# Running maximum of the gated memory spread by one-pass products of split halves; token scales turned to columns through all 128 rows

## The chip, the cores and the metric

One core of one Trainium2 chip. The metric is device microseconds of one execution, the median of three runs. The kernel runs a whole two-part transformer forward pass over 512 tokens; nothing is left to the host but laying the data out.

## The reference, cut to what matters

The first block is an attention block with a feed-forward part, the second block (run twice, layers `l` = 0 and 1) has a SwiGLU part, a mixer of three branches, and another SwiGLU part. The change touches two things in it.

The gated memory (`_mlstm`, 4 heads of 128 channels) is a causal product with gates. Per head and token there is an input gate `ig` and a log forget gate `lf`. With `F` the running sum of `lf`, the weight of key token s for query token t is

```
exp(ig[s] - F[s] - max over u <= t of (ig[u] - F[u], 0))
```

so each head needs the running maximum `M[t]` of `a = ig - F`, and it needs it for every one of the 128 partitions that hold key tokens, along a free axis of 512 query tokens.

The token scales are `rsqrt(mean(x*x) + eps)` of a normalisation, one number per token. In the kernel activations lie with channels on partitions and tokens on the free axis, except for the attention values, which lie with tokens on partitions. There the same scale is needed as a column, `[128 tokens, 1]` for each of the four token blocks.

## The kernel before

Everything is float32. Large products are made of two rounded halves: a weight block and an activation are each a high half and a low half of type fp32r (which TensorE takes in one pass), and three one-pass products (high·high, high·low, low·high) accumulate in one PSUM bank. Products of plain float32 operands leave two matmul records each in the trace, transposes one.

The weights come in 386 units of 8 blocks of 128x128 over one queue (SyncE). For each unit ScalarE makes the high half (L1679, one 128x1024 instruction) and GpSimd the low half (L1992, four 128x256 instructions), two units ahead at most. TensorE walks through the blocks in the order of `plan()`.

The order of all engines' instructions is written by a planner at build time. `Schedule.put` appends a step to one list and also runs it on five model clocks (`class Planned`), with a price for each instruction. Small chains (an attention item, a normalisation) are generators that yield what they wait for; `Schedule.pump` advances one when the planned time of what it waits for has come, and so its TensorE steps land between the steps of a dense group. The prices that matter here: a matmul is 0.013 us plus 0.00167 us a column for float32 and 0.000417 us a column for fp32r, a transpose is 0.11 us. Every engine then issues its own instructions in the order of that list and waits at semaphores where the data isn't there.

The parts that the change touches:

- `columns` (TensorE, matmuls through L721 as all `mm`; VectorE copy L1127) turns a row into columns. The scale tile has the same row in all 128 partitions; the step reads partition 0 alone, four products of `[1,128]` by `[1,1]`. It is called six times: twice at the start (`("rc", 1)`, `("rc", 2)`; the second with a strided view, every fourth token), once in each mixer for the value scale (`("rc", s)`), and once in each mixer for the low-rank branch (`("low", l)`).
- `fgate_in`, `fgate_log`, `fgate_max` (VectorE, L1439 to L1458) work on 4 partitions, one a head: the gate, the two scans, the maximum `Mr` in tile T[3]. `fgate_out` transposes `a` and `M + F` to columns, `fgate_cols` copies them (L1468).
- `ml_m` (TensorE) spreads row h of `Mr` over 128 partitions with a float32 product: stationary `sel_t[0:4, ...]`, which has -1 in row h, moving `Mr`, 4 rows by 512. VectorE copies the bank (L1551) and ScalarE exponentiates. It runs four times in each mixer: heads 0 and 1 one right behind the other, heads 2 and 3 later, each when the PSUM pair of an earlier head has been read (`ml_open`, L1615).
- `sel_t` is loaded once with the second block's masks; it shares its memory with a mask of the first block.

Of the kernel before, what the change touches and what calls it, by code (L numbers as in the profile page):

```python
# [8 lines left out]
F32R = mybir.dt.float32r  # L9
# [6 lines left out]
S = 512  # L16
# [491 lines left out]
def build_program(nc, w, xT, cols, pos, c128, dmask, smask, cmask, sel, vbias, out, stop=None):  # L508
# [5 lines left out]
    with st:  # L514
# [50 lines left out]
        sel_t = at(top[0] + 2 * KB, 512)  # L565
        top[0] += 4 * KB
        R0 = top[0]
        top[0] += 110 * KB
# [18 lines left out]


        SUMS = {n: banks_t[:, 0:512 // n, 512 - n:512] for n in (128, 256)}

        def pair(slot):
            return 2 + 2 * slot, 3 + 2 * slot
# [48 lines left out]
        KR, KRT, KRS = SM[64:128, :], L1[64:128, :], L2[64:128, :]  # L641
        fz, fq = L1[0:4, :], L2[0:4, :]
        lf, Fr, zeros = PADT[0:4, 0:512], PADT[0:4, 512:1024], PAD2[0:4, 0:512]
        ar, FM, Mr = L1[0:4, :], L2[0:4, :], L3[0:4, :]
        acol, fcol = small_t[:, 32:48], small_t[:, 48:64]

        MLS = [[small_t[:, o + 4 * k:o + 4 * k + 4] for k in range(6)] for o in (64, 88)]
# [65 lines left out]
        def tensor_program(pe, need):  # L713
# [82 lines left out]
            def columns(name, b, o, src, view, dst, tok):  # L796

                need.wait_ge(*tok[0].at(tok[1]))
                if o == 0:
                    free(b)  # L800
                    bank[b] = [(v_norm, ("cols", name))]
                for c in range(4):
                    ins = mm(B[b][:, o + c:o + c + 1], view(src, c)[0:1], C["ones"][0:1, 0:1])
                ins.then_inc(*t_stat.next(("cols", name)))

            def head_sum(hid):
# [206 lines left out]
            def ml_m(l, h):  # L1013
                ba = pair(ml_at[l, h][0])[0]
                need.wait_ge(*v_attn.at(("fgate_m", l)))
                need.wait_ge(*in_cm.at("cm"))
                free(ba)
                mm(B[ba], sel_t[0:4, 128 * h:128 * h + 128], Mr).then_inc(*t_attn.next(("ml_m", l, h)))
                bank[ba] = [(v_attn, ("ml_m", l, h))]

            def ml_scores(l, h, j):
# [41 lines left out]
        def vector_program(v, need):  # L1063
# [61 lines left out]
            def columns(name, b, o, src, view, dst, tok):  # L1125
                need.wait_ge(*t_stat.at(("cols", name)))
                v.tensor_copy(dst, B[b][:, o:o + 4]).then_inc(*v_norm.next(("cols", name)))  # L1127

            def turns1():
                need.wait_ge(*in_const.at("const"))  # L1130
                need.wait_ge(*in_cols.at("cols"))
                for k in (1, 2):
                    v.tensor_reduce(SIGN[k], C[f"perm{k}"], AX, A_, negate=True).then_inc(*v_norm.next(("signs",)))
                for n, width in GAINS:
                    v.tensor_scalar(col(n), col(n), -0.5 / width, None, M_).then_inc(*v_norm.next())
                need.wait_ge(*v_norm.last())
                for n, width in GAINS[:4]:
                    v.stream_shuffle(TURNED[n], col(n), SHUFFLE[1]).then_inc(*v_norm.next(("turns1",)))

            def turns2():  # L1140
                for n, width in GAINS[4:]:
# [311 lines left out]

            def fgate_max(l):
                need.wait_ge(*v_attn.at(("fgate_a", l)))
                v.tensor_tensor_scan(Mr, ar, ar, 0.0, MX, MX).then_inc(*v_attn.next(("fgate_m", l)))
                need.wait_ge(*v_attn.last())
                v.tensor_tensor(FM, Mr, Fr, A_).then_inc(*v_attn.next(("fgate_f", l)))  # L1458

            def fgate_out(l, slot):  # L1460
                fgate_bank[l] = pair(slot)[0]
# [162 lines left out]
            def merge2(l, m, gs, tl, bz):  # L1624
# [13 lines left out]
                else:  # L1638
# [4 lines left out]
            return {"whalf": half_weights, "norm": norm, "norm_halves": norm_halves, "norm_squares": norm_squares, "stats": stats, "cols": columns, "turns1": turns1, "turns2": turns2,  # L1643
                    "rope_angles": rope_angles, "values1": values1, "proj": proj, "head_in": head_in, "key_rope": key_rope,
                    "head_rope": head_rope, "head_newton": head_newton, "dil_soft": dil_soft, "dil_norm": dil_norm,
                    "dil_pt": dil_pt, "swa_soft": swa_soft, "swa_norm": swa_norm, "swa_out": swa_out,
                    "halves1": halves1, "merge1": merge1_, "res": residual, "part": part, "relu2": relu2,
                    "relu2_halves": relu2_halves, "ff_a": ff_a, "ff_g": ff_g, "values2": values2,
                    "sb_keep": sb_keep, "sb_split": sb_split, "sb_sum": sb_sum, "sb_out": sb_out,
                    "fgate_in": fgate_in, "fgate_log": fgate_log, "fgate_max": fgate_max, "fgate_out": fgate_out,  # L1650
                    "stats_beside": stats_beside, "consts": consts, "values1_strided": values1_strided,
                    "values2_ml": values2_ml,
                    "fgate_cols": fgate_cols, "low_halves": low_halves, "low_rs": low_rsqrt, "conv": conv, "kup": kup,
# [324 lines left out]
        def pool_program(p, need):  # L1978

            def half_weights(u):  # L1980
                if u not in FRONT:
                    low_quarters(u, range(4))

            def half_weights_rest(u):
                low_quarters(u, (2, 3))

            def low_quarters(u, quarters):
                need.wait_ge(*w_high.at(u))
                hl = whl[u % 2]
                for q in quarters:  # L1990
                    c = slice(256 * q, 256 * q + 256)
                    p.tensor_tensor(hl[:, 1024:2048][:, c], wraw[u % 3][:, c], as_f32(hl[:, c]),  # L1992
                                    ALU.subtract).then_inc(*w_low.next((u, q)))

            def head_out(hid):
                H = heads[hid]
                a, b_, c = H["tiles"][H["slot"]]
                need.wait_ge(*v_attn.at(("normed", hid)))
                need.wait_ge(*H["base"][0].at(H["base"][1]))
                p.tensor_tensor(H["R"], b_, a, ALU.mult).then_inc(*p_attn.next(("head", hid)))  # L2000

            def low_squares(l):
                cq = branch[l]["cq"]
                reach(need, cq[0], *branch[l]["lay"])
                p.tensor_tensor(LS1, YL[0], YL[0], ALU.mult).then_inc(*p_attn.next())
                reach(need, cq[1])
                p.tensor_tensor(LS2, YL[1], YL[1], ALU.mult).then_inc(*p_attn.next())
                need.wait_ge(*p_attn.last())
                p.tensor_tensor(LS1, LS1, LS2, ALU.add).then_inc(*p_attn.next(("low_q", l)))
                need.wait_ge(*p_attn.last())  # L2010
                reach(need, cq[2])
                p.tensor_tensor(LS2, YL[2], YL[2], ALU.mult).then_inc(*p_attn.next(("low_kv", l)))

            return {"whalf": half_weights, "whalf_rest": half_weights_rest, "head_out": head_out, "low_squares": low_squares,
                  "mark": lambda name: mark_of("p", name)}


# [141 lines left out]
        def values_item(slot):  # L2159
            yield "t", (v_norm, ("acc", 0, 7))  # L2160
            put("mark", ("stats", 0))
            put("stats_beside", 0, 128)
            yield "t", (v_norm, ("rstd", 0))
            put("cols", ("rc", 1), 0, 384, rstdB, natural, rcol_t[:, 0:4], (v_norm, ("rstd", 0)))
            put("cols", ("rc", 2), 1, 384, rstdB, strided, rcol_t[:, 4:8], (v_norm, ("rstd", 0)))
            yield "v", (t_stat, ("cols", ("rc", 2)))
            put("values1")
            yield "v",
            put("rope_angles", 1)
            yield "a", (v_norm, ("coangle", 1))  # L2170
            put("rope_table", 1)
# [199 lines left out]
        def swiglu(l, k):  # L2371
# [4 lines left out]
            for i in range(11):  # L2376
                b1, b2 = sch.bank(), sch.bank()
                g1 = sch.dense("fa", b1, xmov(s), freed=(v_evac, ("ff_a", l, k, i)))
                if i == 0:
                    g2 = sch.dense("fg", b2, xmov(s), before=due(s), freed=(v_evac, ("ff_g", l, k, i)))  # L2380
                a, c = sch.tile(), sch.tile()
                put("ff_a", l, k, i, g1, a, busy(a, ((v_evac, ("ff", l, k, i)),)))
                if i:
                    g2 = sch.dense("fg", b2, xmov(s), freed=(v_evac, ("ff_g", l, k, i)))
                if l == 0 and k == 1 and i == 3:
                    put("rope_angles", 2)
                    put("rope_table", 2)
                    put("turns2")
                put("ff_g", l, k, i, g2, a, c, busy(c, ((v_evac, ("ff_y", l, k, i)),)))
                movs.append((HF[i][:, 0:S], HF[i][:, S:2 * S], (v_evac, ("ff", l, k, i))))  # L2390
            put("explog")
# [3 lines left out]
        def mixer(l):  # L2395
# [9 lines left out]
            put("mark", ("stats", s))  # L2405
            put("stats_beside", s, 256)

            def values_item(slot):
                yield "t", (v_norm, ("rstd", s))
                put("cols", ("rc", s), 0, 256, rstdB, natural, rcol_t[:, 0:4], (v_norm, ("rstd", s)))  # L2410
                yield "v", (t_stat, ("cols", ("rc", s)))
                put("values2", l)

# [51 lines left out]
            def gate_item(slot):  # L2465
# [5 lines left out]
                put("fgate_max", l)  # L2471
                yield "t", (v_attn, ("fgate_f", l))
                put("fgate_out", l, slot)
                yield "v", (t_attn, ("fgate", l))
                put("fgate_cols", l)

            def low_item(slot):
# [8 lines left out]
                yield "a", (t_attn, ("low_kv", l))  # L2486
                put("low_rs", l)
                yield "t", (v_attn, ("low_kv", l))
                put("cols", ("low", l), pair(slot)[0], 0, RKV, natural, rcol_t[:, 4:8], (v_attn, ("low_kv", l)))
                sch.done.add(("low", l))  # L2490

            conv_busy, n_conv = {7: lay, 8: lay, 9: lay}, [0]
# [376 lines left out]
```

## Time and profile before

| | us |
|---|---|
| median of 3 runs | 2406.74 |
| lowest and highest | 2405.58, 2408.32 |
| profiled execution, span from first to last instruction | 2406.4 |
| PE busy in it | 2379.8 |
| PEld (weight loads, beside PE) | 1924.6 |
| POOL busy | 1316.2 |
| DVE busy | 1209.2 |
| ACT busy | 965.8 |

The profile gives the profiled execution by its span; the median of the timed runs is 0.3 us above it. PE is TensorE's matmuls, PEld its weight loads, DVE is VectorE, ACT is ScalarE, POOL is GpSimd, SP is SyncE. Busy is the union of an engine's instructions in time. A matmul record is longer than the step to the next one, since matmuls overlap in the array; what a product costs is the step from one start to the next.

### The profile page before, as it was taken

How to read it: one execution, taken by the hardware profiler on the slowest of the kernel's cores; microseconds unless marked ns; L12 is line 12 of the kernel's file. 1: busy time of each engine (PE TensorE's matmuls, PEld its weight loads, DVE VectorE, ACT ScalarE, POOL GpSimd, SP SyncE). 2: the span in 40 equal slices, each digit the busy share in tenths (PEclk: the TensorE clock that was granted, in tenths of full speed). 3: DMA queues.
4: the chain of work that ended last, by engine and by line, in shares of the span. 5: the costliest groups of instructions: out<-in, count | busy, mean ns of one | idle time of the engine just before them, and what ended most of it. 6: DMA issues, size and time to landing. Idle time of an engine off the chain costs nothing.

```text
span 2406.4 us, 29717 instructions
## 1 busy us (share of the span) xinstructions
PE 2379.8 (99%) x11108; PEld 1924.6 (80%) x11108; DVE 1209.2 (50%) x1961; ACT 965.8 (40%) x1513; POOL 1316.2 (55%) x1589
## 2 busy tenths in 40 slices
PE   8999999999999999999999999999999999999999
PEld 8777778888888888777787888888887777788887
DVE  5997765423224432379625743333325785266331
ACT  4554444322223223566524432332336764344321
POOL 5763246656556655366244765555554562466554
PEclk9999999999999999999999999999999999999999
DMA  5321123333333333222122333333332221223333
GB/s 166 109 71 53 47 77 97 96 97 97 97 97 110 97 97 103 71 72 69 54 87 79 97 97 97 96 97 97 97 98 67 72 78 53 88 87 98 96 97 96
DMA packets 59758, 213.40 MB, mean 89 GB/s; under 512 B 6624, under 2 KB 6752, under 8 KB 59488
## 3 DMA queue, kind: packets, MB, share of 16 engines
q1 hardware_dynamic: 59472, 211.38, 29.2%
q8 instruction: 88, 1.44, 0.2%
q14 instruction: 54, 0.44, 0.1%
q10 hardware_dynamic: 144, 0.14, 0.0%
HBM read 209.39 MB, written 2.10 MB: 88 GB/s over the span
## 4 chain that ended last, share of the span: by engine, by line
PE 91%; DVE 6%; issue 1%; ACT 1%; DMA 0%; POOL 0%; SPq 0%; DVEq 0%; ACTq 0%
PE banks L721 89%; DVE t L1203 1%; DVE t L1211 1%; DVE t L1213 1%; DVE t L1488 1%; DVE t L1204 1%; DVE t L1197 1%; DVE t L1219 0%; PE banks L841 0%; PE banks L995 0%; DVE t L1222 0%; ACT t L1679 0%; DMA t<-in_w 0%; PE banks L875 0%; POOL t L1992 0%
## 5 line engine op out<-in xcount | busy, mean ns | idle before, releaser
L721 PE MATMUL banks<-t,t 128*128 128x512 f32 (+4 forms) x10788 | 2351.7, 387 | 17.2 <-ACT t L1699 5.9
L721 PEld LDWEIGHTS banks<-t,t 128*128 128x128 f32 (+2 forms) x10788 | 1889.5, 188 | 452.2 <-issue 64.3
L1992 POOL TENSOR_TENSOR t<-t,t 128x256 fp32r<-128x256 f32 x1544 | 1258.9, 846 | 1049.9 <-ACT t L1679 1041.5
L1679 ACT ACTIVATE t<-t 128x1024 fp32r<-128x1024 f32 x385 | 408.2, 1060 | 1078.8 <-issue 605.5
L1197 DVE TENSOR_TENSOR t<-banks,t 128x512 f32<-128x512 f32 x121 | 83.1, 687 | 169.8 <-PE banks L721 169.2
L1378 DVE TENSOR_TENSOR t<-banks,t 128x512 f32<-128x512 f32 x44 | 30.4, 690 | 184.5 <-PE banks L721 184.3
L1346 DVE SCALAR_TENSOR_TENSOR t<-banks,t 128x512 f32<-128x512 f32 x32 | 22.1, 691 | 155.4 <-PE banks L721 155.4
L1080 DVE SCALAR_TENSOR_TENSOR t<-t,t,t 128x512 fp32r<-128x512 f32 x64 | 52.0, 817 | 58.1 <-ACT t L1699 58.1
L1323 DVE TENSOR_TENSOR t<-t,t 128x512 fp32r<-128x512 f32 x68 | 70.5, 1036 | 2.3
L1352 DVE TENSOR_TENSOR t<-banks,t 128x512 f32<-128x512 f32 x24 | 16.6, 691 | 106.0 <-PE banks L721 106.0
L1699 ACT ACTIVATE t<-t,t 128x512 fp32r<-128x512 f32 x64 | 45.6, 715 | 55.7 <-DVE t L1346 49.1
L2000 POOL TENSOR_TENSOR t<-t,t 128x512 f32<-128x512 f32 x33 | 49.6, 1506 | 29.7 <-DVE t L1222 29.7
L1373 DVE TENSOR_TENSOR t<-banks,t 128x512 f32<-128x512 f32 x44 | 30.4, 691 | 70.3 <-PE banks L721 69.9
L1093 DVE TENSOR_TENSOR t<-t,t 128x512 f32<-128x512 f32 x56 | 59.4, 1061 | 3.1 <-ACT t L1705 3.1
L1321 DVE CAST t<-t 128x512 fp32r<-128x512 f32 x68 | 55.3, 813 | 2.5
L1358 DVE SCALAR_TENSOR_TENSOR t<-banks,t 128x512 f32<-128x512 f32 x32 | 22.1, 691 | 65.2 <-PE banks L721 65.1
L1344 DVE TENSOR_TENSOR t<-banks,t 128x512 f32<-128x512 f32 x32 | 22.1, 690 | 56.6 <-PE banks L721 56.6
L1488 DVE SCALAR_TENSOR_TENSOR t<-t,t,t 128x511 f32<-128x511 f32 (+2 forms) x48 | 46.7, 972 | 7.1 <-ACT t L1887 6.3
L1715 ACT ACTIVATE t<-t 128x512 f32<-128x512 f32 x45 | 28.5, 633 | 33.4 <-DVE t L1213 32.5
L1710 ACT ACTIVATE t<-banks,t 128x512 f32<-128x512 f32 x45 | 30.6, 681 | 22.5 <-PE banks L721 22.4
L1098 DVE SCALAR_TENSOR_TENSOR t<-banks,t 128x512 f32<-128x512 f32 x12 | 8.3, 692 | 57.8 <-ACT t L1715 57.7
L1705 ACT ACTIVATE t<-t 128x512 f32<-128x512 f32 x56 | 34.6, 617 | 4.8 <-DVE t L1093 4.8
(182 smaller groups left out, 1304.7 us busy)
## 6 DMA issues: line engine op xcount, KB each, us to landing
t<-in_w SPq DMA_DIRECT2D x386, 512.0 KB, 3.5
t<-in_xT SPq DMA_DIRECT2D x8, 256.0 KB, 5.7
out<-t SPq DMA_DIRECT2D x8, 256.0 KB, 4.5
t<-in_dmask SPq DMA_DIRECT2D x1, 1536.0 KB, 7.7
t<-in_vbias SPq DMA_DIRECT2D x2, 384.0 KB, 4.1
t<-in_c SPq DMA_DIRECT2D x1, 576.0 KB, 8.6
t<-in_w SPq DMA_DIRECT2D x2, 256.0 KB, 3.9
t<-in_pos SPq DMA_DIRECT2D x2, 256.0 KB, 4.1
```

What stands on the lines that cost most here:

```text
L721: return pe.matmul(o, l, r, start=start, stop=stop, skip_group_check=True)
L1080: v.scalar_tensor_tensor(out=XL[m], in0=X[m], scalar=g, in1=as_f32(XH[m]), op0=M_, op1=S_).then_inc(*v_norm.next(("xl", s, m)))
L1093: v.tensor_tensor(acc, acc, sqt, A_).then_inc(*v_norm.next(("acc", s, m)))
L1197: v.tensor_tensor(G.dst, B[G.bank], rstdB, M_).then_inc(*v_evac.next(("proj", g)))
L1321: v.tensor_copy(hi, src).then_inc(*v_evac.next())
L1323: v.tensor_tensor(lo, src, as_f32(hi), S_).then_inc(*v_evac.next(name))
L1488: v.scalar_tensor_tensor(out=dst[:, tap:S], in0=T[k][:, 0:S - tap], scalar=cols_t[:, cw + 3 - tap:cw + 4 - tap], in1=dst[:, tap:S], op0=M_ ...
L1679: a.activation(whl[u % 2][:, 0:1024], wraw[u % 3][:, :], ACT.Copy).then_inc(*w_high.next(u))
L1699: a.activation(XH[m], X[m], ACT.Copy, scale=col(STAGE[s], m)).then_inc(*a_norm.next(("high", s, m)))
L1705: a.activation(sqt, X[m], ACT.Square).then_inc(*a_norm.next(("square", s, m)))
L1992: p.tensor_tensor(hl[:, 1024:2048][:, c], wraw[u % 3][:, c], as_f32(hl[:, c]), ALU.subtract).then_inc(*w_low.next((u, q)))
L2000: p.tensor_tensor(H["R"], b_, a, ALU.mult).then_inc(*p_attn.next(("head", hid)))
```

## The change

`Mr` is no longer read by TensorE. VectorE rounds it to fp32r into rows 0 to 3 of a new 128-row tile `Mhl` and writes the remainder to rows 32 to 35 (`fgate_halves`); the other 120 rows are zeroed by GpSimd once in each mixer (`fgate_zero`). `sel` is copied to rows 32 to 35 as well and rounded to fp32r in place, once (`select`, VectorE, in the first SwiGLU part behind `turns2`). `ml_m` is then one fp32r product of 128 rows, which adds high and low half. `Mr` moves to the tile that held `lf`, `Mhl` takes the place of T[3].

`columns` reads all 128 rows. For the two calls at the start (result one column wide) it is a float32 product with the first column of the identity as moving operand; for the other four it is a transpose of the 128x128 block, of which VectorE copies the first column.

```diff
+        TURNS = banks_t[:, 0:4, 256:384]
+        def few(b):
+            return B[b][:, 384:388].rearrange("p (c n) -> p c n", c=4)
+        def whole(b):
+            return B[b].rearrange("p (c n) -> p c n", c=4)
...
-        ar, FM, Mr = L1[0:4, :], L2[0:4, :], L3[0:4, :]
+        ar, FM, Mr = L1[0:4, :], L2[0:4, :], PADT[0:4, 0:512]
+        Mhl = reg(94, S, F32R)[:, :]
...
-                if o == 0:
+                if b is not None:
                     free(b)
                     bank[b] = [(v_norm, ("cols", name))]
                 for c in range(4):
-                    ins = mm(B[b][:, o + c:o + c + 1], view(src, c)[0:1], C["ones"][0:1, 0:1])
+                    if to.shape[2] == 1:
+                        ins = mm(to[:, c, :], view(src, c), C["ident"][:, 0:1])
+                    else:
+                        ins = pe.transpose(to[:, c, :], view(src, c), C["ident"])
...
             def ml_m(l, h):
-                need.wait_ge(*in_cm.at("cm"))
+                need.wait_ge(*v_norm.at(("sel",)))
                 free(ba)
-                mm(B[ba], sel_t[0:4, 128 * h:128 * h + 128], Mr).then_inc(*t_attn.next(("ml_m", l, h)))
+                mm(B[ba], sel_r[:, 128 * h:128 * h + 128], Mhl).then_inc(*t_attn.next(("ml_m", l, h)))
...
-                v.tensor_copy(dst, B[b][:, o:o + 4]).then_inc(*v_norm.next(("cols", name)))
+                v.tensor_copy(dst, to[:, :, 0]).then_inc(*v_norm.next(("cols", name)))
...
+            def select():
+                need.wait_ge(*in_cm.at("cm"))
+                v.tensor_copy(sel_t[32:36, :], sel_t[0:4, :]).then_inc(*v_norm.next())
+                need.wait_ge(*v_norm.last())
+                v.tensor_copy(sel_r[:, :], sel_t[:, :]).then_inc(*v_norm.next(("sel",)))
...
+            def fgate_halves(l):
+                need.wait_ge(*v_attn.at(("fgate_f", l)))
+                need.wait_ge(*p_attn.at(("fgate_zero", l)))
+                v.tensor_copy(Mhl[0:4, :], Mr).then_inc(*v_attn.next())
+                need.wait_ge(*v_attn.last())
+                v.tensor_tensor(Mhl[32:36, :], Mr, as_f32(Mhl[0:4, :]), S_).then_inc(*v_attn.next(("fgate_m", l)))
...
+            def fgate_zero(l):
+                reach(need, *branch[l]["lay"])
+                p.memset(as_f32(Mhl), 0.0).then_inc(*p_attn.next(("fgate_zero", l)))
...
-            put("cols", ("rc", 1), 0, 384, rstdB, natural, rcol_t[:, 0:4], (v_norm, ("rstd", 0)))
-            put("cols", ("rc", 2), 1, 384, rstdB, strided, rcol_t[:, 4:8], (v_norm, ("rstd", 0)))
+            put("cols", ("rc", 1), None, few(0), rstdB, natural, rcol_t[:, 0:4], (v_norm, ("rstd", 0)))
+            put("cols", ("rc", 2), None, few(1), rstdB, strided, rcol_t[:, 4:8], (v_norm, ("rstd", 0)))
...
                     put("turns2")
+                    put("select")
...
             put("stats_beside", s, 256)
+            put("fgate_zero", l)
...
-                put("cols", ("rc", s), 0, 256, rstdB, natural, rcol_t[:, 0:4], (v_norm, ("rstd", s)))
+                put("cols", ("rc", s), None, TURNS, rstdB, natural, rcol_t[:, 0:4], (v_norm, ("rstd", s)))
...
                 put("fgate_out", l, slot)
+                put("fgate_halves", l)
...
-                put("cols", ("low", l), pair(slot)[0], 0, RKV, natural, rcol_t[:, 4:8], (v_attn, ("low_kv", l)))
+                put("cols", ("low", l), pair(slot)[0], whole(pair(slot)[0]), RKV, natural, rcol_t[:, 4:8], (v_attn, ("low_kv", l)))
```

## Rows read from the trace of the kernel before

**Rows 1.** Page, part 1: busy time, share and instructions of each engine

```profile
PE 2379.8 (99%) x11108; PEld 1924.6 (80%) x11108; DVE 1209.2 (50%) x1961; ACT 965.8 (40%) x1513; POOL 1316.2 (55%) x1589
```

**Rows 2.** Page, part 4: share of the span by engine

```profile
PE 91%; DVE 6%; issue 1%; ACT 1%; DMA 0%; POOL 0%; SPq 0%; DVEq 0%; ACTq 0%
```

**Rows 3.** PE's waits: for whom, us in total, times, longest

```profile
PE banks L721 <- DVE t L1615: 2.3, 2, 1.1
```

**Rows 4.** PE by line and shape: count, busy us, mean ns, idle before

```profile
L721 PE MATMUL banks<-t,t 4*128 4x512 f32 x16 | 8.4, 627 | 2.3 <-DVE t L1615 2.3
L721 PE MATMUL banks<-t,t 1*128 1x1 f32 x48 | 7.1, 268 | 0.0
```

**Rows 5.** Stretch of dense products: length, then busy (count) of each engine, PEclk

```profile
1500.00:1550.00 50.00, 50.00 (x222) 41.46 (x221) 17.50 (x22) 14.98 (x17) 29.52 (x38) 1.00 0.33 96
```

**Rows 6.** PEld in time, layer 0, head 2: start, length, operation, idle

```profile
1199.79 0.19 PEld L721 LDWEIGHTS banks<-t,t 128*128 128x128 f32 x1
1200.35 0.29 PEld L721 LDWEIGHTS banks<-t,t 4*128 4x128 f32 x2 [0.37 <-issue]
1201.40 0.77 PEld L721 LDWEIGHTS banks<-t,t 128*128 128x128 f32 x4 [0.76 <-issue]
```

**Rows 7.** PEld in time, layer 1, heads 0 and 1, then head 2

```profile
2000.81 0.42 PEld L721 LDWEIGHTS banks<-t,t 128*128 128x128 f32 x2
2001.60 0.29 PEld L721 LDWEIGHTS banks<-t,t 4*128 4x128 f32 x2 [0.36 <-issue]
...
2003.51 0.53 PEld L721 LDWEIGHTS banks<-t,t 128*128 128x128 f32 x3 [0.76 <-issue]
...
2023.29 0.29 PEld L721 LDWEIGHTS banks<-t,t 4*128 4x128 f32 x2 [0.37 <-issue]
```

**Rows 8.** PE by shape between 38.6 and 41.2 us, the two first calls

```profile
L721 PE MATMUL banks<-t,t 1*128 1x1 f32 x16 | 2.9, 307 | 0.0
```

**Rows 9.** PE in time: four 128x128 transposes of `ml_turn`

```profile
1199.12 0.60 PE L1051 MATMUL banks<-t,t 128*128 128x128 f32 x4
```

**Rows 10.** Stretches at, ahead of and without a lower clock (columns of Rows 5)

```profile
1179.90:1183.30 3.40, 3.40 (x8) 1.80 (x7) 1.89 (x5) 1.57 (x7) 0.00 (x0) 0.50 0.18 72
1272.10:1275.50 3.40, 3.40 (x10) 2.65 (x9) 1.29 (x2) 1.32 (x3) 0.00 (x0) 0.51 0.19 72
2094.70:2098.10 3.40, 3.40 (x9) 2.62 (x9) 0.76 (x2) 1.09 (x3) 0.00 (x0) 0.51 0.23 93
1176.50:1179.90 3.40, 3.40 (x11) 1.66 (x10) 1.72 (x6) 0.62 (x2) 1.04 (x2) 1.00 0.23 82
1268.70:1272.10 3.40, 2.26 (x7) 0.97 (x6) 2.07 (x3) 3.37 (x6) 1.03 (x2) 0.99 0.38 87
...
184.00:192.00 8.00, 5.39 (x22) 3.20 (x21) 7.66 (x18) 4.61 (x10) 4.93 (x6) 1.00 0.22 66
```

**Rows 11.** PEld in time, layer 0, head 0

```profile
1177.01 0.29 PEld L721 LDWEIGHTS banks<-t,t 4*128 4x128 f32 x2 [0.36 <-issue]
```

**Rows 12.** DVE by line and shape

```profile
L1321 DVE CAST t<-t 128x512 fp32r<-128x512 f32 x68 | 55.3, 813 | 2.5
L1452 DVE TENSOR_TENSOR t<-t,t 4x512 f32<-4x512 f32 x2 | 2.1, 1036 | 0.1
L1439 DVE COPY t<-t 4x512 f32<-4x512 f32 x2 | 1.7, 846 | 0.1
```

**Rows 13.** Stretches around the gates' scans in layer 0 (columns of Rows 5)

```profile
1030.00:1040.00 10.00, 10.00 (x45) 7.49 (x44) 9.80 (x14) 7.99 (x15) 6.38 (x6) 1.00 0.18 52
...
1050.00:1060.00 10.00, 10.00 (x55) 8.46 (x55) 4.66 (x9) 6.82 (x13) 7.97 (x10) 1.00 0.24 64
```

**Rows 14.** DVE in time, behind the second rope table

```profile
810.74 0.69 DVE L1378 TENSOR_TENSOR t<-banks,t 128x512 f32<-128x512 f32 x1 [3.88 <-PE banks L721]
```

**Rows 15.** POOL by line and shape

```profile
L2012 POOL TENSOR_TENSOR t<-t 128x512 f32<-128x512 f32 x2 | 2.1, 1040 | 0.2
```

**Rows 16.** POOL in time, end of layer 0's value products

```profile
949.25 2.83 POOL L1992 TENSOR_TENSOR t<-t,t 128x256 fp32r<-128x256 f32 x4 [2.95 <-ACT t L1679]
```

More of the change, by code:

```diff
@@ L564, in build_program @@
         cm_t = at(top[0], 512)
-        sel_t = at(top[0] + 2 * KB, 512)
+        sel_t, sel_r = at(top[0] + 2 * KB, 512), at(top[0] + 2 * KB, 512, F32R)
         top[0] += 4 * KB
@@ L794, in stats_beside, with columns @@
                 ins.then_inc(*t_stat.next(("stats", s)))
-            def columns(name, b, o, src, view, dst, tok):
+            def columns(name, b, to, src, view, dst, tok):
                 need.wait_ge(*tok[0].at(tok[1]))
-                if o == 0:
+                if b is not None:
                     free(b)
@@ L1123, in consts, with columns @@
                         *v_norm.next(("consts",)))
-            def columns(name, b, o, src, view, dst, tok):
+            def columns(name, b, to, src, view, dst, tok):
                 need.wait_ge(*t_stat.at(("cols", name)))
-                v.tensor_copy(dst, B[b][:, o:o + 4]).then_inc(*v_norm.next(("cols", name)))
+                v.tensor_copy(dst, to[:, :, 0]).then_inc(*v_norm.next(("cols", name)))
             def turns1():
@@ L1455, in fgate_max @@
                 need.wait_ge(*v_attn.at(("fgate_a", l)))
-                v.tensor_tensor_scan(Mr, ar, ar, 0.0, MX, MX).then_inc(*v_attn.next(("fgate_m", l)))
+                v.tensor_tensor_scan(Mr, ar, ar, 0.0, MX, MX).then_inc(*v_attn.next())
                 need.wait_ge(*v_attn.last())
                 v.tensor_tensor(FM, Mr, Fr, A_).then_inc(*v_attn.next(("fgate_f", l)))
+            def fgate_halves(l):
[4 more added lines that the diff above has]
+                v.tensor_tensor(Mhl[32:36, :], Mr, as_f32(Mhl[0:4, :]), S_).then_inc(*v_attn.next(("fgate_m", l)))
             def fgate_out(l, slot):
@@ L1641, in merge2 @@
                 split(MH[m][0], MH[m][1], T[tl[0]], ("mixed", l, m))
-            return {"whalf": half_weights, "norm": norm, "norm_halves": norm_halves, "norm_squares": norm_squares, "stats": stats, "cols": columns, "turns1": turns1, "turns2": turns2,
+            return {"whalf": half_weights, "norm": norm, "norm_halves": norm_halves, "norm_squares": norm_squares, "stats": stats, "cols": columns, "turns1": turns1, "turns2": turns2, "select": select,
                     "rope_angles": rope_angles, "values1": values1, "proj": proj, "head_in": head_in, "key_rope": key_rope,
@@ L1649, in vector_program @@
                     "sb_keep": sb_keep, "sb_split": sb_split, "sb_sum": sb_sum, "sb_out": sb_out,
-                    "fgate_in": fgate_in, "fgate_log": fgate_log, "fgate_max": fgate_max, "fgate_out": fgate_out,
+                    "fgate_in": fgate_in, "fgate_log": fgate_log, "fgate_max": fgate_max, "fgate_halves": fgate_halves, "fgate_out": fgate_out,
                     "stats_beside": stats_beside, "consts": consts, "values1_strided": values1_strided,
@@ L2012, in low_squares @@
                 p.tensor_tensor(LS2, YL[2], YL[2], ALU.mult).then_inc(*p_attn.next(("low_kv", l)))
-            return {"whalf": half_weights, "whalf_rest": half_weights_rest, "head_out": head_out, "low_squares": low_squares,
+            return {"whalf": half_weights, "whalf_rest": half_weights_rest, "head_out": head_out, "low_squares": low_squares, "fgate_zero": fgate_zero,
                   "mark": lambda name: mark_of("p", name)}
```

## The prediction, on record before the changed kernel was timed

> **What bounds the kernel now.** I read the page's busy times first: TensorE is busy for 2379.8 of 2406.4 us [rows 1], the next engine for 1316.2. The chain that ended last is TensorE for 91% [rows 2]. Then TensorE's own waits: two of 1.1 us each stand ahead of a product that this change touches, `ml_m` of head 3 [rows 3]. So the kernel is a queue of matmuls, and a microsecond taken out of that queue comes off the time unless a wait grows for it. Two views tell what the touched products cost: PE by shape, and the weight loads in order of time, whose starts follow the products one by one. Last I read the granted clock in short stretches, because the page's slices of 60 us hide three short falls.
>
> **What `ml_m` costs and will cost.** Eight products of 4 rows by 512 columns leave 16 records and 8.4 us busy, 1.05 us each [rows 4]. In a dense stretch 222 products of 128 rows by 512 columns pass in 50 us, 0.225 us each [rows 5]. From load to load, with the joints included: for a single one the load of a dense product starts at 1199.79, the 4-row load at 1200.35 and the next full one at 1201.40; 1.61 us hold two dense products (the load of the second left no record) and one `ml_m`, so it takes 1.61 - 0.45 = 1.16 us [rows 6]. For the pair, 2000.81 to 2003.51 holds three dense products (the two recorded loads of that row and one more up to 2001.60) and two `ml_m`: 2.70 - 0.68 = 2.02 us [rows 7]. The new `ml_m` is an fp32r product of 128 rows by 512, the dense kind, 0.225 us. It saves 0.93 us each where it is alone and 2.02 - 0.45 = 1.57 us a pair. Each mixer has one pair and two single ones: 1.57 + 1.86 = 3.4 us, 6.9 us for two. Bounds: at the busy figure alone, without joints, 8 x (1.05 - 0.225) = 6.6 us; the first full-row product behind a 4-row one may be slow too, which these differences don't catch, so I add 0.1 us for each of the six places as an estimate from the 0.11 us by which the joint ahead of the single one is longer than a dense step (1200.35 - 1199.79 = 0.56 against two steps of 0.225): 0.6 us. I take 7.5, between 6.6 and 8.
>
> **What the columns cost.** 48 records of one row, 7.1 us busy [rows 4]; the 16 of the two calls at the start are 2.9 of it [rows 8], so the other four calls take 4.2 / 4 = 1.05 us each. Four transposes of 128x128 take 0.60 us [rows 9]. Four calls save 4 x 0.45 = 1.8 us, up to 2.6 if the joints with one-row products cost 0.1 us at each end as above; I take 2.1. The two calls at the start stay products with one moving column and the same 128 columns of weights, from 128 rows where there was one. No row here shows that form; I take no difference. It can gain the joints (0.3 us); the other end is the rate doubling, 2.9 us.
> The Trainium skill ("TensorE: Matmul & The Clock Gate", section on LDWEIGHTS) has a load's time go by its columns and not its rows. By that this term is nothing, as taken; the 4-row and 1-row loads of the trace cannot show it for the strided view.
>
> **The clock.** The granted clock is 1.00 nearly everywhere, and 0.50 or 0.51 (1.2 instead of 2.4 GHz) in three stretches: from 1179.9, 1272.1 and 2094.7 us, each seen for 3.4 us [rows 10]. Each comes right behind 4-row products. Ahead of the first PE is busy for 3.40 of 3.40 us, with the pair of `ml_m` in it, ahead of the second for 2.26 of 3.40, the wait for L1615 and one `ml_m` in it [rows 10]; the third is like the second. Waits alone didn't do it: from 184 to 192 us PE is busy for 5.39 of 8.00 us, the most broken stretch of the kernel, at 1.00. Nor does each 4-row product: the pair of layer 1 passes at full clock. From the pair to head 2, layer 0 needs 1200.35 - 1177.01 = 23.34 us and layer 1, same work, 2023.29 - 2001.60 = 21.69 us [rows 6, 7, 11]: one fall costs 1.65 us. My reading is that a product with 4 of 128 rows fills the array too little to hold the clock. With those gone what stays ahead of heads 3 is a 1.1 us wait, less than the waits at 184 us which cost no fall. So I expect all three to go: 3 x 1.65 = 4.95 us; bounds 0 and 4.95.
> The Trainium skill (same page, section "PE-mode transpose") says that a transpose doesn't count as PE-busy as a matmul does, which speaks against turning columns by transposes. By it the calls could bring falls of their own (rival 2). The trace bears this out little: 0.60 us of transposes [rows 9] take the place of 1.05 us of one-row products, and none of the three falls follows transposes alone.
>
> **What is added.** `fgate_halves` is a cast and a subtraction of 4x512, 0.85 and 1.04 us [rows 12], twice in all, and it falls where VectorE is at 9.80 of 10 us [rows 13]. Behind it in VectorE's queue stand the evictions of the dense groups (two banks take turns there) and the halves for the stick-breaking sums. TensorE has no wait in these stretches (10.00 of 10), and 10 to 20 us later VectorE is down to 4.66 of 10, so 1.9 us of backlog is worked off before a bank is missed; I take nothing. Uncovered it is 2 x 1.9 = 3.8 us. `select` is one 4-row copy and one cast of 128x512, 0.85 + 0.81 us [rows 12], behind the rope table in a SwiGLU stage with eight banks in turn, where VectorE then sits idle for 3.88 us [rows 14]: nothing, and once. Its data are the last of three loads issued together 30 us before. `fgate_zero` is one 128x512 fill on GpSimd, at most the 1.04 us of an operation of two operands on the same shape [rows 15]; it stands between two units' low halves, where GpSimd is idle for 2.95 us [rows 16]. Its wait is for the end of the stage before, which those low halves' own unit waits for anyway. Nothing. VectorE's copies of the columns read the same four numbers, at a stride. No DMA is added or moved.
>
> **The order.** The planner prices `ml_m` at 0.87 us before and 0.23 after, and a call of columns at 0.06 before and 0.44 after. Both come nearer to the trace (1.05 and 0.225; 1.05 and 0.60), so its clock is off by less. But the lists change from the first call on, and some chain step will sit one place nearer to what it waits for, or farther. The nearest row is the wait for L1615, 1.1 us; I count two of them either way as range and nothing in the sum.
>
> **Sum.** 7.5 + 2.1 + 4.95 = 14.6 us off the profiled execution's 2406.4, which is 2391.8; the median of the runs is 0.3 above that span, so 2392.1.
>
> **The rivals.**
> 1. *The falls stay or partly stay.* The two in front of heads 3 have a wait in them, and only half of what precedes them goes. For it: 1.1 us of idleness remains at the same place. Against it: the 184 us stretch. Time with two falls left: 2392.1 + 3.3 = 2395.4; with all three, 2397.1. The Trainium skill (same page, closing table) ties a lower clock to idle gaps between bursts; products with few rows aren't named. By that alone the change moves no fall; the trace disagrees at 1179.9, where PE had not been idle.
> 2. *Transposes hold the clock no better than few-row products.* Then a call of columns could bring a fall where the one-row form brought none. Against it: the four transposes of [rows 9] and the softmax items' own brought none. Four falls at worst: 2392.1 + 6.6 = 2398.7.
> 3. *VectorE's added 1.9 us a mixer isn't covered.* For it: 9.80 of 10 us. Against it: PE without a wait for 30 us behind. Time: 2392.1 + 3.8 = 2395.9.
> 4. *The other side: the new order.* Each mixer has eight softmax items and four memory items, each with about six hand-overs between engines, placed by planned times. If the reshuffle puts a step ahead of its data in every second item, that is 12 waits more at 1.1 us, 13 us, and with the falls left in (5 us) the time is 2410. It decides from 14.6 / 1.1 = 13 such waits on with the falls gone, 9 with the falls left; the kernel has two of this kind now. Nothing in the trace speaks for so many.
> 5. *The change doesn't do what it says:* the 128-row product might not run in one pass (1.05 us as now). Then 7.5 and most of the clock's part are lost: 2406.7 - 2.1 = 2404.6. Against it: the same types and shape run at 0.225 us [rows 5].
>
> **How the numbers follow.** Forecast as summed, all falls gone, 0.60; falls left 0.20; transposes with falls 0.02; VectorE uncovered 0.10; new order slower 0.02; not one pass 0.01; the rest, 0.05, is a gain larger than summed (waits that vanish, 2388 to 2390). The range takes the forecast, the falls left, VectorE uncovered and both signs of two waits: 2389 to 2398. What a measurement can tell from no change is 0.2%, 4.8 us: below 2401.9 is faster. Faster 0.95, same 0.03, slower 0.02.
>
> **What would show it.** Eight 4x512 products gone and eight more 128x512 in one record each, the next load 0.23 us behind; 32 one-row records gone for 16 transposes at some 0.6 us a call; the two calls at the start at 2.9 us still. The granted clock at 1.00 around heads 0 and 3; 21.7 less 0.4 us from the pair to head 2 in both layers. PE's busy time down by 14 us with its waits in sum unchanged. Wrong would be: falls at other places, PE waits for VectorE between 1045 and 1080 us, or a span that falls by under 9 us.

## The result, and the profile after

| | before | after |
|---|---|---|
| median | 2407.53 (4 runs) | 2396.88 (4 runs) |
| lowest to highest | 2405.58 to 2409.01 | 2396.29 to 2397.56 |
| profiled execution, span | 2406.4 | 2394.4 |

The ratio is 0.9955, 95% interval [0.9943, 0.9966]: 10.65 us faster. The forecast was 2392.1 with a range of 2389 to 2398; the time lies in the range, 4.8 us above the forecast. The profiled execution of the changed kernel took 2396.29 us, so 1.9 us lie around its span and not the 0.3 us of the forecast.

Medians of different sets are compared below where a variant is set against the changed kernel; the kernel before has medians from 2406.84 to 2408.23 us in these sets, so such a difference is uncertain by about as much. Where it matters, the spans of the profiled executions are given beside it.

The busy times of the page, to be read against [rows 1]: TensorE lost 12.3 us of busy time, as much as the span lost.

```profile
PE 2367.5 (99%) x11084; PEld 1919.7 (80%) x11084; DVE 1212.7 (51%) x1967; ACT 965.6 (40%) x1513; POOL 1325.5 (55%) x1591
```

TensorE by line and shape, against [rows 4] and [rows 8]: the 4x512 group is gone, the start calls cost the same 2.8 us with 128 rows as with one, and the four other calls are 16 transposes.

```profile
L729 PE MATMUL banks<-t,t 128*128 128x1 f32 x16 | 2.8, 306 | 0.0
L814 PE MATMUL banks<-t,t 128*128 128x128 f32 x16 | 2.5, 279 | 0.5 <-DVE t L1113 0.5
```

Stretches of the changed kernel, columns as in [rows 5]: behind the start calls, around heads 0 and 1 of layer 0, and around the wait of head 3.

```profile
38.50:42.40 3.90, 3.90 (x22) 3.90 (x21) 1.32 (x6) 1.06 (x1) 2.62 (x4) 0.99 0.41 134
42.40:45.80 3.40, 3.40 (x9) 2.75 (x9) 3.29 (x10) 0.00 (x0) 0.18 (x1) 0.51 0.55 157
1176.40:1179.80 3.40, 3.40 (x17) 2.54 (x17) 2.08 (x6) 0.71 (x2) 1.80 (x3) 1.00 0.22 28
1265.00:1268.40 3.40, 2.26 (x10) 1.58 (x9) 2.07 (x3) 3.37 (x6) 1.03 (x2) 1.00 0.35 99
```

The last of these has the same 2.26 us of 3.40 as the stretch ahead of the second fall in [rows 10], and ten matmul records where there were seven. It keeps the clock. All three falls of [rows 10] (stretches at half the clock) are gone; one has come at 42.4 us, right behind the sixteen records of one-column products of the start calls. The forecast had named a fall at another place as a sign of being wrong.

TensorE's waits (for whom, us in total, times, longest), against [rows 3]. The wait for `ml_open` is as before. A new one has 1.0 us a mixer, for the eviction of a dense group; the transposes of the low branch wait 0.3 us a call for the scale.

```profile
PE banks L729 <- DVE t L1639: 2.3, 2, 1.1
...
PE banks L729 <- DVE t L1214: 1.9, 2, 1.0
...
PE banks L814 <- DVE t L1113: 0.5, 2, 0.3
```

TensorE and VectorE of the changed kernel in time there, in layer 0: start, length, idle and releaser in brackets.

```profile
1071.46 0.66 PE L814 MATMUL banks<-t,t 128*128 128x128 f32 x4 [0.27 <-DVE t L1113]
...
1079.24 0.98 PE L729 MATMUL banks<-t,t 128*128 128x512 f32 x3 [0.97 <-DVE t L1214]
1080.90 4.32 PE L729 MATMUL banks<-t,t 128*128 128x512 f32 x16 [0.69 <-DVE t L1520]
```
```profile
1072.59 5.99 DVE L1512 SCALAR_TENSOR_TENSOR t<-t,t,t 128x509 f32<-128x509 f32 x6
1078.50 0.69 DVE L1214 TENSOR_TENSOR t<-banks,t 128x512 f32<-128x512 f32 x1
```

And the same place in the kernel before:

```profile
1074.48 3.03 DVE L1488 SCALAR_TENSOR_TENSOR t<-t,t,t 128x511 f32<-128x511 f32 x3 [1.77 <-ACT t L1887]
1077.47 0.69 DVE L1197 TENSOR_TENSOR t<-banks,t 128x512 f32<-128x512 f32 x1
```
```profile
1080.25 4.10 PE L721 MATMUL banks<-t,t 128*128 128x512 f32 x15 [1.07 <-DVE t L1496]
```

Six taps of the convolution (L1512) stand ahead of the eviction L1214, where three stood ahead of it before (L1488, L1197). That is the planner's doing. TensorE had one wait here before, of 1.07 us, and has three now, 0.27 + 0.97 + 0.69 = 1.93 us; in layer 1 they are 1.95 us where 1.42 stood. So the net loss at this place is 1.4 us for both layers, less than the new waits by themselves. Waits for VectorE between 1045 and 1080 us were the forecast's second sign of being wrong; the kernel before has none there. All of TensorE's idle time together is nearly the same, 26.9 us against 26.6 (span less busy time).

### The profile page after: what moved, and what is told of

It is laid out like the page before. It is cut to its first block, busy times and chain, and to the rows that moved or that the text cites. A ratio compares the mean times of both kernels' runs of the same rounds, so it can differ in the third digit from the quotient of the medians.

```text
span 2394.4 us, 29678 instructions
## 1 busy us (share of the span) xinstructions
PE 2367.5 (99%) x11084; PEld 1919.7 (80%) x11084; DVE 1212.7 (51%) x1967; ACT 965.6 (40%) x1513; POOL 1325.5 (55%) x1591
## 4 chain that ended last, share of the span: by engine, by line
PE 90%; DVE 7%; issue 1%; ACT 1%; POOL 1%; DMA 0%; SPq 0%; ACTq 0%; DVEq 0%
PE banks L729 88%; DVE t L1512 1%; DVE t L1220 1%; DVE t L1228 1%; DVE t L1230 1%; DVE t L1214 1%; POOL t L2016 1%; DVE t L1221 1%; DVE t L1236 0%; PE banks L852 0%; PE banks L1006 0%; ACT t L1703 0%; DVE t L1239 0%; PE banks L886 0%; DMA t<-in_w 0%
## 5 line engine op out<-in xcount | busy, mean ns | idle before, releaser
L729 PE MATMUL banks<-t,t 128*128 128x512 f32 (+6 forms) x10748 | 2338.2, 386 | 17.0 <-ACT t L1723 6.1
L1214 DVE TENSOR_TENSOR t<-banks,t 128x512 f32<-128x512 f32 x121 | 83.1, 687 | 159.9 <-PE banks L729 159.3
L1363 DVE SCALAR_TENSOR_TENSOR t<-banks,t 128x512 f32<-128x512 f32 x32 | 22.1, 692 | 155.4 <-PE banks L729 155.4
L1375 DVE SCALAR_TENSOR_TENSOR t<-banks,t 128x512 f32<-128x512 f32 x32 | 22.1, 691 | 65.2 <-PE banks L729 65.1
L1512 DVE SCALAR_TENSOR_TENSOR t<-t,t,t 128x511 f32<-128x511 f32 (+2 forms) x48 | 49.0, 1025 | 3.7 <-ACT t L1911 2.8
L1361 DVE TENSOR_TENSOR t<-banks,t 128x512 f32<-128x512 f32 x32 | 22.1, 690 | 56.6 <-PE banks L729 56.6
```

What stands on the lines that cost most here:

```text
L729: return pe.matmul(o, l, r, start=start, stop=stop, skip_group_check=True)
L1214: v.tensor_tensor(G.dst, B[G.bank], rstdB, M_).then_inc(*v_evac.next(("proj", g)))
L1512: v.scalar_tensor_tensor(out=dst[:, tap:S], in0=T[k][:, 0:S - tap], scalar=cols_t[:, cw + 3 - tap:cw + 4 - tap], in1=dst[:, tap:S], op0=M_ ...
```

## The experiments

Each is timed in five rounds beside the kernel before (the two with idle products in one). "Below" is against the median of before in the same set.

### Which half of the change brings the time

`mlm_only` is the changed kernel with `columns` and its six calls as they were:

```diff
-                    if to.shape[2] == 1:
-                        ins = mm(to[:, c, :], view(src, c), C["ident"][:, 0:1])
-                    else:
-                        ins = pe.transpose(to[:, c, :], view(src, c), C["ident"])
+                    ins = mm(B[b][:, o + c:o + c + 1], view(src, c)[0:1], C["ones"][0:1, 0:1])
```

> Only the gated memory's part of the change (one-pass product of 128 rows, halves, zeroing, select); the token scales are turned with one row as before. Theory A (few-row products cost their passes and joints, and also the clock; the new planned order gives some back): the products bring 7.5 us, the three falls of the clock near heads 0 and 3 go (4.95 us), the new order costs 1.5 to 2.5 us, so 10 to 11 us below before, and no fall at all in the mixers. Theory B (the falls have nothing to do with rows): 5 to 6 us below before, with falls left near the same places.

Measured 2397.09 us against 2407.54, ratio 0.9957 [0.9945, 0.9970]: 10.45 us below, and no fall in its trace, though its start calls are one-column products too. The mean clock of the traced run is 1.000 and of the four others 0.999, as in traces with one fall or two, so the others most likely have one. `cols_only` is the reverse, the kernel before with the new `columns` and its calls.

> Only the token scales' part (all 128 rows; transposes in the mixers, one moving column at the start); ml_m as before in float32 with 4 rows. Theory A: four calls save 2.1 to 3 us, the three falls stay, the fall behind the two calls at the start (42.4 us in the changed kernel) may be there too, since it goes by the one-column products and not by the rows: 0.5 to 3 us below before. Theory B (the fall at 42 us came from somewhere else): 2 to 3 us below before without a fall there.

Measured 2405.64 us against 2407.54, ratio 0.9994 [0.9985, 1.0002]: 1.9 us below by the medians, which the interval does not tell from nothing. By the spans, with three falls in each, it is 2.7 us (2403.7 against 2406.4). Its `ml_m` still have 4 rows, and three stretches at half clock are there again, two of them at the same heads as in [rows 10], the first of layer 1 at the pair that had passed unharmed before. None is at 42 us this time, right behind the start calls:

```profile
1269.40:1272.80 3.40, 3.40 (x10) 2.66 (x9) 1.47 (x3) 1.42 (x3) 0.00 (x0) 0.50 0.16 59
1999.90:2003.30 3.40, 3.40 (x7) 1.96 (x6) 1.66 (x5) 1.69 (x6) 0.00 (x0) 0.51 0.22 89
2092.00:2095.40 3.40, 3.40 (x9) 2.63 (x8) 0.81 (x2) 1.12 (x3) 0.00 (x0) 0.50 0.23 89
39.00:42.40 3.40, 3.40 (x20) 3.40 (x19) 0.83 (x4) 1.06 (x1) 2.14 (x4) 1.00 0.50 154
```

So most of the gain is `ml_m`, and the falls of the mixers go with it.

### Rows or passes

The new `ml_m` differs from the old in two things. `rows128_4pass` keeps the rows and goes back to float32; the planner still sees the new price, so the order is that of the changed kernel:

```diff
-                mm(B[ba], sel_r[:, 128 * h:128 * h + 128], Mhl)
+                s_, m_ = sel_r[:, 128 * h:128 * h + 128], Mhl
+                if not isinstance(pe, Planned):
+                    s_, m_ = as_f32(s_), as_f32(m_)
+                mm(B[ba], s_, m_)
```

> The changed kernel, order and all, but TensorE reads the same 128-row operands as plain float32, so ml_m takes several passes again with all rows filled. Theory A: 8 x (0.86 - 0.225) = 5.1 us above the changed kernel, 5.5 us below before, no falls in the mixers: rows hold the clock, passes cost time. Theory B (falls come with the length of the float32 product, not with its rows): 7 to 10 us above the changed kernel, with one to three falls near ml_m.

Measured 2401.37 us against 2407.54, ratio 0.9972 [0.9962, 0.9982]: 6.2 us below before and 4.5 us above the changed kernel, near the 5.1 expected. By the spans it is 5.9 us above, of which one fall more is 1.65. The stretch around heads 0 and 1 holds the clock with the long products in it (first row below). One fall follows the start calls at 41.5 us and one comes at 1901.8 us, behind a stretch in which TensorE works for 1.83 of 3.40 us (last two rows), with no `ml_m` near. This is the place of the new waits in layer 1, 0.97 and 0.70 us:

```profile
1176.00:1183.00 7.00, 7.00 (x28) 4.33 (x27) 2.88 (x8) 2.25 (x8) 2.69 (x4) 1.00 0.25 75
1901.80:1905.20 3.40, 3.40 (x8) 1.99 (x7) 2.02 (x3) 3.27 (x6) 0.00 (x0) 0.51 0.53 154
1898.40:1901.80 3.40, 1.83 (x7) 1.25 (x8) 2.09 (x4) 2.04 (x4) 2.80 (x4) 0.99 0.28 108
```

Theory A holds at `ml_m`; the prediction's "Waits alone didn't do it" doesn't hold in general. The waits that the new order brought can cost a fall of their own. In the changed kernel the same place has 1.95 us of work in 3.40 and in the kernel before 1.88, both at 1.00.

`rows36_1pass` keeps the single pass and contracts only the rows that hold data:

```diff
-                mm(B[ba], sel_r[:, 128 * h:128 * h + 128], Mhl)
+                mm(B[ba], sel_r[0:36, 128 * h:128 * h + 128], Mhl[0:36, :])
```

> The changed kernel, but the one-pass product contracts rows 0 to 35 alone instead of all 128. Theory A: each product is 0.225 us and one joint of up to 0.1 us on either side: 0 to 1.6 us above the changed kernel, no falls, since so short a product can't empty the array for long. Theory B (each product with few rows costs much whatever its passes): 4 us and more above the changed kernel.

Measured 2398.33 us (2395.63 to 2400.79), ratio 0.9960 [0.9946, 0.9974], 1.4 us above the changed kernel by the medians and not apart from it by the intervals. No fall in the mixers, one at 43.1 us. Once the product is in one pass, no cost of its few rows is seen.

### The dose

To see the clock's cause by itself, four idle float32 products go ahead of each `ml_m` into the same bank, unseen by the planner, with 4 rows in `dose4rows` and with 128 in `dose128rows`:

```diff
+                if not isinstance(pe, Planned):
+                    for _ in range(4):
+                        mm(B[ba], as_f32(sel_r)[0:4, 128 * h:128 * h + 128], as_f32(Mhl)[0:4, :])
```

> The changed kernel with four idle float32 products of 4 rows by 512 columns ahead of each ml_m, same order (their result is overwritten). Theory A (few rows lose the clock): 8 x 4 x 0.43 x 2 = 27.5 us of products and joints of 0.2 us each, and a fall at nearly each of the eight places, in which these products themselves take twice as long: 38 to 50 us above the changed kernel, with 6 or more falls. Theory B (rows don't matter): 27 to 30 us above, with no more falls than the same products of 128 rows.

> The same with idle float32 products of all 128 rows by 512 columns. Theory A: 27 to 28 us above the changed kernel and no fall at these eight places. Theory B (long float32 products lose the clock whatever their rows): as many falls as with 4 rows.

Measured 2447.78 us (2 runs) and 2425.09 us (2 runs), against 2407.95: 50.9 and 28.2 us above the changed kernel, the first just above the 38 to 50 expected. The same number of products, 8 x 4, costs 22.7 us more with 4 rows than with 128. With 4 rows the clock is at one half in six stretches near `ml_m`, up to 13.6 us on end, though TensorE does not pause at all in them; with 128 rows it is at 1.00 there. The six stretches add up to 44.2 us (13.6, two of 10.2, three of 3.4); at half speed they lose up to 22.1 us, so they can account for nearly all of the 22.7. Two of the six, then the same places of the other kernel, and last its one fall:

```profile
1182.00:1195.60 13.60, 13.60 (x22) 6.63 (x22) 2.47 (x7) 2.10 (x7) 0.00 (x0) 0.50 0.00 1
1287.90:1298.00 10.10, 10.10 (x19) 5.45 (x18) 1.17 (x3) 1.82 (x3) 0.00 (x0) 0.50 0.11 44
```
```profile
1182.00:1196.00 14.00, 14.00 (x67) 10.60 (x66) 6.70 (x20) 4.77 (x18) 2.80 (x4) 1.00 0.11 30
1286.00:1300.00 14.00, 14.00 (x73) 11.84 (x72) 7.54 (x18) 5.73 (x16) 5.89 (x7) 1.00 0.25 76
1910.60:1914.00 3.40, 3.40 (x8) 1.99 (x7) 2.02 (x3) 3.28 (x6) 0.10 (x1) 0.50 0.57 154
```

The fall of `dose128rows` at 1910.6 us stands behind the same waits of layer 1 as that of `rows128_4pass`, with 1.73 us of work in 3.40 ahead of it and no `ml_m` near. At `ml_m` this settles it: long float32 products of 4 rows lose the clock, with the engine busy throughout, and the same products of 128 rows, 120 of them zeros, don't.

### The order

`order_kept` runs every instruction of the changed kernel, but tells the planner the old prices. One of its edits (the fill, `select` and `columns` likewise):

```diff
+                now = getattr(v, "now", None)
                 v.tensor_copy(Mhl[0:4, :], Mr).then_inc(*v_attn.next())
...
+                if isinstance(v, Planned):
+                    v.now = now
```

> The changed kernel with every instruction of it, but the planner is told the old prices (0.87 us for ml_m, 0.015 us for each column product, nothing for the added halves, fill and select), so the steps stand in the order of the kernel before. Theory A (the new order brought new waits in front of the key products, 1.0 us a mixer, and for the six taps of the convolution put ahead of an eviction): 1.5 to 2.5 us below the changed kernel, some 12.5 us below before. Theory B (the order is neutral and the missing gain is the added vector work itself, or the fall of the clock at the start): within 0.5 us of the changed kernel.

Measured 2394.89 us against 2407.95, ratio 0.9945 [0.9932, 0.9959]; its five runs (2394.34 to 2395.66) all lie below the four of the changed kernel, 2.0 us by the medians, as expected by theory A. But by the mean clock (1.000) two of the five have no fall at the start, and all four of the changed kernel have one. The spans of the two traced runs, with one fall each, are 2393.7 and 2394.4: with the fall alike the order costs 0.7 us, and 1.3 by the medians of the runs at 0.999. The taps ahead of the eviction are three again, 3.03 us, and the wait for it is gone, with the one wait of the kernel before back in its place:

```profile
1073.88 3.03 DVE L1523 SCALAR_TENSOR_TENSOR t<-t,t,t 128x511 f32<-128x511 f32 x3 [1.77 <-ACT t L1922]
1076.88 0.69 DVE L1222 TENSOR_TENSOR t<-banks,t 128x512 f32<-128x512 f32 x1
...
1079.65 6.58 PE L729 MATMUL banks<-t,t 128*128 128x512 f32 x24 [1.07 <-DVE t L1531]
```

That saves 1.7 us at this place in both layers. What it loses elsewhere is the wait of `ml_turn`'s transposes, 1.0 us more than in the changed kernel (its row first, then the changed kernel's):

```profile
PE banks L1067 <- DVE t L1642: 2.1, 4, 0.5
PE banks L1062 <- DVE t L1631: 1.1, 2, 0.5
```

The added vector work runs in it all the same, so that work is covered, as forecast; its price moved the steps. Which price? `halves_unpriced` makes only that edit, `mlm_unpriced` only gives `ml_m` its old price.

> The changed kernel where the planner is told alone that the halves of the maximum cost nothing (they still run). Theory A (the harm is in pricing 1.4 us of vector work in a full stretch, which moves the convolution's six taps ahead of an eviction): TensorE's 1.0 us wait for L1214 in each mixer is gone and the time is 1.5 to 2.2 us below the changed kernel. Theory B (the harm comes from the price of ml_m): the waits stay, within 0.4 us of the changed kernel.

> The changed kernel where the planner is told the old price of ml_m alone (0.87 us). Theory A: the waits for L1214 stay, within 0.4 us of the changed kernel. Theory B: 1.5 to 2.2 us below it.

Measured 2393.22 us against 2408.23 (0.9942 [0.9928, 0.9955]) and 2397.69 us (0.9958 [0.9946, 0.9971]). `mlm_unpriced` keeps the six taps and the wait of 0.97 us, and it has the 1.0 us more at `ml_turn` too. It is 0.8 us above the changed kernel by the medians and 1.4 by the spans, outside the 0.4 of expectation A: by the spans the new price of `ml_m` is a small gain, and it is not the harm. `halves_unpriced` has four taps and a wait of 0.71 us, and the waits of the low branch's transposes are gone: the wait became shorter and did not go, so this part of expectation A failed. Of its five runs three stand at a mean clock of 1.000 and two at 0.999, so some of its 3.7 us is the fall at the start that came less often. Its traced run has no fall and a span of 2391.0 us; with one fall's 1.65 added it is 1.75 below the changed kernel, inside the 1.5 to 2.2 expected of the price alone. The fourth tap goes with the price of the columns: `cols_only`, where the planner sees only that price change, has four taps and the same wait, 0.71 us.

### The start

`start_turned` turns the two start calls by transposes too, the second behind the copy of the first:

```diff
-            put("cols", ("rc", 1), None, few(0), ...)
-            put("cols", ("rc", 2), None, few(1), ..., (v_norm, ("rstd", 0)))
+            put("cols", ("rc", 1), None, FIRST4, ...)
+            yield "t", (v_norm, ("cols", ("rc", 1)))
+            put("cols", ("rc", 2), None, FIRST4, ..., (v_norm, ("cols", ("rc", 1))))
```

> The changed kernel, but the two calls at the start are four transposes each too, the second behind the copy of the first. Theory A (the fall at 42.4 us comes from sixteen one-column products in a row): no fall there, products 2.9 us down to some 1.6, so 1 to 3 us below the changed kernel. Theory B (the fall comes from the pauses of the first 17 us, or transposes hold the clock as badly): the fall stays, 0 to 1 us below, or above where TensorE waits for the copy.

Measured 2393.01 us against 2407.95, ratio 0.9937 [0.9925, 0.9950], 3.9 us below the changed kernel and more than the 1 to 3 expected; by the spans it is 3.3, which is one fall and the shorter products. The 2.8 us of one-column products are two times 0.6 us, and all five runs have a mean clock of 1.000:

```profile
38.26 0.60 PE L815 MATMUL banks<-t,t 128*128 128x128 f32 x4
...
41.65 0.63 PE L815 MATMUL banks<-t,t 128*128 128x128 f32 x4
```

`both` joins this with `order_kept`, `halves_start` joins it with `halves_unpriced`.

> The changed kernel with the order of the kernel before (old prices in the planner) and the two start calls as transposes. If the two gains are of different places and add up (2.2 us and 3.9 us below the changed kernel), 2390.8 to 2391.5, some 16 us below before; if the start's gain was partly the order's, 2393.

> The changed kernel with the two start calls as transposes and the halves of the maximum unpriced in the planner. If the two gains (3.9 us by the start, of which up to 1.7 is the fall; 3 us by the price, of which a part is that the fall stayed away in three of its five runs) add without the fall counted twice: 2390.5 to 2391.5, 17 us below before; if not, 2392.8 as with the whole old order.

Measured 2392.79 us against 2408.23 (0.9938 [0.9926, 0.9951]) and 2391.95 us against 2406.84 (0.9938 [0.9924, 0.9951]). Neither is clearly below `start_turned`, and neither reaches the sum of the two gains. In the medians of `order_kept` and `halves_unpriced` a part of the gain was the start's fall, absent in two and three of their runs, and it can't be gained twice. `halves_start` is the fastest, 14.9 us below before, and by the ratios not told apart from the other two; by the spans it is 2.4 us below `start_turned` (2388.7 against 2391.1) and `both` 0.2.

## Why the prediction was right, and where it was off

The time lies in the range, 4.8 us above the forecast. By the spans the forecast was 2391.8 and the trace has 2394.4: 1.65 us are the fall at the start, 0.7 the order and 0.2 the products. The rest is how a span was turned into a median: 1.6 us by the wrong distance around it, and 0.6 because the traced execution lies below the median of its kernel.

1. **TensorE bounds.** Right: 12.3 us of busy time gone, 12.0 us of span.
2. **The products.** `order_kept` has the old order and one fall where before had three. Its span is 2393.7, 12.7 us below 2406.4; two falls fewer are 3.3 us, so the products brought 9.4 us (9.2 by TensorE's busy time). The terms were 7.5 + 2.1 = 9.6. The sum fits, but not its parts: the columns brought 2.7 to 2.9 us (`cols_only`, span and busy time) and not 2.1, which leaves 6.3 to 6.7 for `ml_m` and not 7.5. The 0.6 us added for a slow product behind a 4-row one is not seen. That the two errors nearly cancel is luck. The passes alone are 4.5 us by the medians of `rows128_4pass`, 4.3 by the spans less its second fall.
3. **The start calls.** Right in their own time: 2.8 us with 128 rows, 2.9 with one [rows 8]. Taking them as indifferent to the clock was wrong.
4. **The clock.** The mechanism was right at `ml_m` and shown by the dose: the three falls go with the 4-row products. It was not whole: falls also came behind one-column products and behind waits. The size was off: "all three to go", 4.95 us, but one came behind the start calls, 1.65 us. I had looked for falls only where the kernel before had them. The kernel before has more or fewer from run to run: of its 45 runs beside the experiments, the nine at a mean clock of 0.999 took 2404.2 to 2406.7 us, the 23 at 0.998 2406.2 to 2408.4, the eleven at 0.997 2408.1 to 2411.6, and two at 0.996 2409.1 and 2410.7.
5. **The order.** "Nothing in the sum" was off by 0.7 us in the spans with the fall alike and by 2.0 in the medians. It is the net of two sides: the price of 1.4 us of planned vector work and of the columns put six taps ahead of an eviction for which TensorE then waited, and the new price of `ml_m`, to which I gave most of the words, saved 1.0 us of waits at `ml_turn`.
6. **The added vector work.** Right: in `order_kept`, where it runs, TensorE is idle for 26.4 us, and for 26.6 in the kernel before. It took 0.41 + 1.10 us a mixer and not 1.9.
7. **What lies around the span.** 1.9 us and not 0.3. The forecast set one execution's span against the median of others; by the 1.9 us the profiled execution of before took 2408.3 us, like the slowest of its first three runs. Reckoned from that, 2408.3 - 14.6 = 2393.7.
8. **From pair to head 2.** 19.4 us in both layers, from copy to copy of the bank, where 21.3 was forecast. That they are equal fits no fall; why the stretch is shorter than forecast was not followed up.

Rival 1 (falls left) was partly true with another fall than it named. Rival 2 (transposes lose the clock) fell: `start_turned` has more of them and no fall. The Trainium skill ("TensorE: Matmul & The Clock Gate", section "PE-mode transpose") says that a transpose does not count as PE-busy in the same way. Here eight in place of sixteen records of one-column products kept the clock in all five runs; groups of four, 0.6 us each between full products, can't tell whether they count less, only that so few cost no fall. Rival 3 fell, and rival 4 is the direction in which the order's 0.7 us went.

What stays open: why the falls behind the start calls and behind the waits of layer 1 come in some runs and not in others. That one-column products cause the first is supported by `start_turned`, which also spreads the two calls apart; the two were not tried one by one.

## What to carry to other kernels

Count a long product that fills few of the array's rows twice, once by its own time and once by the clock it can cost to the work behind it. Filling the rows with zeros cost TensorE nothing that these runs can see. Where a planner orders the work by prices, a change of prices is a change of its own: time it apart, with the new work priced at nothing. And set a span only against another span, with the same number of falls in it.

## What the runs showed of the hardware

- The granted clock stood at one half for up to 13.6 us on end while TensorE was busy for all of it, with idle float32 products of 4 rows by 512 (`dose4rows`), and at 1.00 near the same places with as many of 128 rows (`dose128rows`).
- A float32 product of 4 rows by 512 leaves two loads 0.43 us apart at full clock (`dose4rows`), 0.86 us a product, where an fp32r product of 128 rows by 512 takes 0.225 us [rows 5].
- Sixteen records of one-column products, each behind a load of 128 columns, take 2.8 us from 128 rows and 2.9 from one, the strided view included.
- A one-pass product of 36 rows by 512 has a mean of 470 ns in its record and not the 396 of full ones, and its cost in the median was not told from nothing (`rows36_1pass`).
- A fall also came where no few-row product was near, behind 1.83 us of work in 3.40 (`rows128_4pass`) and 1.73 in 3.40 (`dose128rows`), and none at the same place with 1.88 in the kernel before and 1.95 in the changed one.
